# A chunked recurrence's triangular inverse: from 64x64 products to 32x32 tiles with one joining step

## What is computed

```python
def step(state, inp):
    r_t, w_t, k_t, v_t, kk_t, a_t = inp
    sa = jnp.einsum('bhvk,bhk->bhv', state, -kk_t)
    state = (state * w_t[:, :, None, :] + sa[..., None] * (kk_t * a_t)[:, :, None, :]
             + v_t[..., None] * k_t[:, :, None, :])
    return state, jnp.einsum('bhvk,bhk->bhv', state, r_t)
```

## Time and profile before

| what | value |
|---|---|
| median of 3 runs | 1946.18 us (1941.5 to 1951.0) |
| the profiled execution | 1940.98 us |
| its span, first to last instruction | 1939.2 us |
| mean granted TensorE clock in the span | 0.986 of full speed |
| TensorE busy | 1866.9 us, 96% |
| DVE, ACT, GpSimd busy | 362.0, 260.8, 49.6 us |
| matmuls, and as many weight loads | 19404 |
| from level 0 to the chunk loop, in each layer | 62.53 us |

### The profile page before, as it was taken

The page is one execution under the profiler, slowest core; times in us unless marked ns, Lnnn a source line. Parts: engine busy times, 40 slices in busy tenths (PEclk is TensorE's granted clock), DMA queues, the critical chain, the costliest instruction groups (busy, mean ns, idle before and its releaser), DMA issues.

```text
span 1939.2 us, 42075 instructions
## 1 busy us (share of the span) xinstructions
PE 1866.9 (96%) x19404; PEld 1228.6 (63%) x19404; DVE 362.0 (19%) x760; ACT 260.8 (13%) x514; POOL 49.6 (3%) x98
## 2 busy tenths in 40 slices
PE   6999999999999999999799999999999999999996
PEld 5788878788887778878535445353454535445354
DVE  1355133100001555232310101001010010100102
ACT  1324111100001333120100000100001000100001
POOL 3000200000000001100000000000000000000000
PEclk9999999999999999999799999999999999999998
DMA  6432212443434332221989999999999999999970
GB/s 189 148 130 88 89 45 87 175 172 131 171 112 132 120 108 88 89 84 48 380 335 369 363 366 416 354 373 357 356 399 369 376 357 364 387 370 389 353 267 23
DMA packets 122838, 462.08 MB, mean 238 GB/s; under 512 B 9566, under 2 KB 20496, under 8 KB 106288
## 3 DMA queue, kind: packets, MB, share of 16 engines
q1 hardware_dynamic: 122672, 459.46, 62.8%
HBM read 458.39 MB, written 1.05 MB: 237 GB/s over the span
## 4 chain that ended last, share of the span: by engine, by line
PE 96%; DVE 2%; ACT 1%; DMA 1%; issue 1%; SPq 0%; DVEq 0%; ACTq 0%
PE bank L1002 30%; PE bank L383 25%; PE bank L1028 15%; PE bank L885 4%; PE bank L675 3%; PE bank L845 3%; PE bank L958 2%; PE bank L716 2%; PE bank L832 1%; PE bank L967 1%; PE bank L1013 1%; PE bank L422 1%; PE bank L369 1%; DMA slot<-in_ffn_w_gate 0%; PE bank L759 0%
## 5 line engine op out<-in xcount | busy, mean ns | idle before, releaser
L1002 PE MATMUL bank<-slot,xg 128*32 128x512 f32 (+1 forms) x6144 | 582.1, 539 | 0.0
L383 PE MATMUL bank<-h,slot 128*128 128x256 f32 x2176 | 486.5, 383 | 7.5 <-ACT rel L1454 5.3
L383 PEld LDWEIGHTS bank<-h,slot 128*128 128x128 f32 x2176 | 414.0, 192 | 70.0 <-issue 13.7
L1002 PEld LDWEIGHTS bank<-slot,xg 128*32 128x32 f32 x6144 | 198.4, 110 | 371.0 <-issue 368.9
L1028 PE MATMUL bank<-slot,aT 128*32 128x256 f32 x5376 | 293.4, 379 | 0.0
L1028 PEld LDWEIGHTS bank<-slot,aT 128*32 128x32 f32 x5376 | 173.4, 110 | 115.0 <-issue 2.7
L2125 DVE TENSOR_TENSOR av<-gs,bank 128x512 f32<-128x512 f32 (+1 forms) x48 | 29.8, 621 | 618.2 <-PE bank L1002 618.2
L885 PE MATMUL bank<-hid,slot 128*128 128x256 f32 x352 | 77.0, 379 | 0.9 <-DVE hid L1992 0.9
L885 PEld LDWEIGHTS bank<-hid,slot 128*128 128x128 f32 x352 | 66.9, 190 | 10.2 <-issue 1.2
L1593 ACT ACTIVATE gs<-bank 128x512 f32<-128x512 f32 (+1 forms) x48 | 25.2, 543 | 284.6 <-PE bank L1002 284.5
L1599 ACT ACTIVATE aT<-bank 128x512 f32<-128x512 f32 (+1 forms) x48 | 23.2, 544 | 288.9 <-PE bank L1013 288.9
(11 more groups left out here) (400 smaller groups left out, 1190.3 us busy)
## 6 DMA issues: line engine op xcount, KB each, us to landing
slot<-in_moe_w_gate SPq DMA_DIRECT2D x32, 2048.0 KB, 11.6
slot<-in_moe_w_up SPq DMA_DIRECT2D x32, 2048.0 KB, 15.5
slot<-in_moe_w_down SPq DMA_DIRECT2D x32, 2048.0 KB, 10.6
slot<-in_moe_w_gate SPq DMA_DIRECT2D x32, 1536.0 KB, 7.7
slot<-in_moe_w_up SPq DMA_DIRECT2D x32, 1536.0 KB, 11.6
slot<-in_moe_w_down SPq DMA_DIRECT2D x32, 1536.0 KB, 8.5
slot<-in_w_in SPq DMA_DIRECT2D x20, 2048.0 KB, 8.2
slot<-in_ffn_w_gate SPq DMA_DIRECT2D x5, 2048.0 KB, 7.8
```

The costliest lines, as they stand in the source:

```text
L383: ins = mm(o, w[:, k, c:c + n], rhs[:, k, :], start=k == 0, stop=k == nk - 1)
L1002: ins = mm(banks[b0 + g][32 * p:32 * p + 32, 0:width], xg[:, k, 32 * g:32 * g + 32], w[:, kk, p * width:(p + 1) * width], start=k == 0, st ...
```

## The change

The inverse up to blocks of 32 (levels 0 to 4) is kept compactly. A 64x64 chunk inverse has, up to that level, only two 32x32 diagonal blocks, so Ti, Tt and Xs become [128, 16, 32]: partitions in quarters of 32, 16 = 2 token tiles x 8 heads. `blocks` makes a product for both token tiles at once in one bank: 16 x 4 matmuls of 32x32, quarter r of the partitions with quarter r of the output. In level 0, x0 and y0 are Lo's blocks against a 32x32 identity and the other way about. Levels 1 to 4 have x, z and y as before, with the gate halves where they were. Lo keeps its full width, and GpSimd's masks of a level now wait for one bank (y0, then x) and TensorE for both masks.

Level 5 becomes the join: `xl` multiplies the off-diagonal 32x32 block of Bm with Ti, 32 matmuls over two banks; ACT and DVE evacuate one bank each; then the first filler; then `zl`, 32 matmuls over two banks, from Xs and Tt. The wide result Tf is put together from clears (GpSimd, twice, in level 0), copies of Tt (GpSimd twice, ACT once, DVE once) and the two evacuations of zl, and TensorE waits for all of these ahead of the chunk loop. SA reads Tf in place of Tt. The set-up makes a 32x32 identity in four more copies.

The core of the diff (left out: the places of the tiles and the semaphore's name):

```diff
@@ -675,15 +677,29 @@
                             ins = mm(b[hs(q), m * HC:(m + 1) * HC], lhs(q, m), rhs(q, m), start=True, stop=True)
                     close_bank(ins, name)
 
-                for lev in range(NLEV):
-                    for tt in range(NT):
-                        need(pe, "lo_ready", (l * NLEV + lev) * NT + tt + 1)
-                        if lev:
-                            for nm in ("y", "z") if lev > 1 else ("x",):
-                                need_sb(pe, f"{l}{nm}{lev - 1}{tt}")
-                        product(f"{l}x{lev}{tt}", tt, lambda q, m: Lo[hs(q), tt, m, :],
-                                lambda q, m: Ti[hs(q), tt, m, :] if lev else id64[hs(q), :])
+                def quarter(r):
+                    return slice(32 * r, 32 * r + 32)
+
+                def low(r, n):
+                    c = 32 * (r % 2)
+                    return Lo[quarter(r), n // 8, n % 8, c:c + 32]
+
+                def blocks(name, lhs, rhs):
+
+                    b = open_bank(pe, name)
+                    for n in range(16):
+                        for r in range(4):
+                            ins = mm(b[quarter(r), 32 * n:32 * n + 32], lhs(r, n), rhs(r, n), start=True, stop=True)
+                    close_bank(ins, name)
+
+                def one(r, n):
+                    return ident[quarter(r), 32 * r:32 * r + 32]
+
+                for lev in range(NLEV - 1):
+                    need(pe, "lo_ready", (l * (NLEV - 1) + lev + 1) * NT)
                     if lev == 0:
+                        blocks(f"{l}x0", low, one)
+                        blocks(f"{l}y0", one, low)
                         for tt in range(NT):
                             need_sb(pe, f"{l}vt{tt}")
                             for g in range(2):
...
@@ -692,17 +708,24 @@
                             product(f"{l}Gv{tt}", tt, lambda q, m: Bm[hs(q), tt, m // 4, m % 4, 2, :],
                                     lambda q, m: vt[hs(q), tt, head(m // 4, m % 4)])
                         continue
-                    if lev < NLEV - 1:
-                        gate_half(5 + lev, 0)
-                    for tt in range(NT):
-                        need_sb(pe, f"{l}x{lev}{tt}")
-                        product(f"{l}z{lev}{tt}", tt, lambda q, m: Xs[hs(q), tt, m, :],
-                                lambda q, m: Tt[hs(q), tt, m, :])
-                        if lev < NLEV - 1:
-                            product(f"{l}y{lev}{tt}", tt, lambda q, m: Tt[hs(q), tt, m, :],
-                                    lambda q, m: Xs[hs(q), tt, m, :])
-                    if lev < NLEV - 1:
-                        gate_half(5 + lev, 1)
+                    need_sb(pe, f"{l}x0" if lev == 1 else f"{l}y{lev - 1}")
+                    blocks(f"{l}x{lev}", low, lambda r, n: Ti[quarter(r), n, :])
+                    gate_half(5 + lev, 0)
+                    need_sb(pe, f"{l}x{lev}")
+                    need_sb(pe, f"{l}y0" if lev == 1 else f"{l}z{lev - 1}")
+                    blocks(f"{l}z{lev}", lambda r, n: Xs[quarter(r), n, :], lambda r, n: Tt[quarter(r), n, :])
+                    blocks(f"{l}y{lev}", lambda r, n: Tt[quarter(r), n, :], lambda r, n: Xs[quarter(r), n, :])
+                    gate_half(5 + lev, 1)
+                need_sb(pe, f"{l}y{NLEV - 2}")
+                need_sb(pe, f"{l}z{NLEV - 2}")
+                xb = [open_bank(pe, f"{l}xl{q}") for q in range(2)]
+                for n in range(16):
+                    for q in range(2):
+                        ins = mm(xb[q][quarter(2 * q + 1), 32 * n:32 * n + 32],
+                                 Bm[quarter(2 * q), n // 8, n % 8 // 4, n % 4, 0, 32:HC], Ti[quarter(2 * q), n, :],
+                                 start=True, stop=True)
+                        if n == 15:
+                            close_bank(ins, f"{l}xl{q}")
 
                 wb = c3(open_slot(pe, L + "pa"), 4, D)
 
...
@@ -731,10 +754,20 @@
                     if not fill:
                         free_slot(L + "pa", f"{l}pd3")
 
+                filler()
+                need_sb(pe, f"{l}xl0")
+                need_sb(pe, f"{l}xl1")
+                zb = [open_bank(pe, f"{l}zl{q}") for q in range(2)]
+                for n in range(16):
+                    for q in range(2):
+                        ins = mm(zb[q][quarter(2 * q), 32 * n:32 * n + 32], Xs[quarter(2 * q + 1), n, :],
+                                 Tt[quarter(2 * q + 1), n, :], start=True, stop=True)
+                        if n == 15:
+                            close_bank(ins, f"{l}zl{q}")
+                need(pe, "t_copied", 6 * (l + 1))
+                need_sb(pe, f"{l}zl0")
+                need_sb(pe, f"{l}zl1")
                 for tt in range(NT):
-                    if tt == 0:
-                        filler()
-                    need_sb(pe, f"{l}z{NLEV - 1}{tt}")
                     need_sb(pe, f"{l}Gv{tt}")
                     need_sb(pe, f"{l}bt{tt}")
                     need_sb(pe, f"{l}kt{tt}")
...
@@ -756,7 +789,7 @@
                     b = open_bank(pe, f"{l}SA{c}")
                     for u in range(2):
                         for j in range(4):
-                            ins = mm(b[hs(q), col(u, j)], Tt[hs(q), tt, 4 * u + j, :],
+                            ins = mm(b[hs(q), col(u, j)], Tf[hs(q), tt, 4 * u + j, :],
                                      Gs[hs(q), col(u, j)] if c else Gv[hs(q), tt, col(u, j)], start=True, stop=True)
                     close_bank(ins, f"{l}SA{c}")
                     if c < NC - 1:
...
@@ -1317,6 +1350,9 @@
                     step(nc.gpsimd.tensor_copy(tri[64:128, i, :], tri128[64:128, i % 2, 64:128]))
                 step(nc.gpsimd.tensor_copy(id64[0:64, :], ident[0:64, 0:64]))
                 step(nc.gpsimd.tensor_copy(id64[64:128, :], ident[64:128, 64:128]))
+                for r in range(4):
+                    o = slice(32 * r, 32 * r + 32)
+                    step(nc.gpsimd.tensor_copy(id32[o, :], ident[o, o]))
                 for lv in range(NLEV):
                     bs = 1 << lv
                     o = lev128[:, lv, :].rearrange("p (n b) -> p n b", b=2 * bs)[:, :, bs:]
...
@@ -1350,19 +1386,30 @@
                     need_sb(gp, f"{l}vt{tt}")
                 for g in range(2):
                     need_sb(gp, f"{l}bo{g}")
-                for lev in range(NLEV):
+                for lev in range(NLEV - 1):
                     for tt in range(NT):
                         if lev == 0:
                             for g in range(2):
                                 for u in range(2):
                                     need_sb(gp, f"{l}B{tt}{g}{u}")
                         elif lev == 1:
-                            need_sb(gp, f"{l}x0{tt}")
+                            take(gp, f"{l}y0")
                         else:
-                            take(gp, f"{l}x{lev - 1}{tt}")
+                            take(gp, f"{l}x{lev - 1}")
                         nc.gpsimd.tensor_tensor(Lo[:, tt, :, :], Bm[:, tt, :, :, 0, :].rearrange("p u j t -> p (u j) t"),
                                                 level[:, lev:lev + 1, :].broadcast_to([P, 8, HC]),
                                                 ALU.mult).then_inc(S["lo_ready"], 1)
+                    if lev == 0:
+                        need(gp, "lo_ready", l * (NLEV - 1) * NT + NT)
+                        for q in range(2):
+                            nc.gpsimd.memset(Tf[64 * q + 32:64 * q + 64, :, :, 0:32], 0.0).then_inc(S["t_copied"], 1)
+                        need(gp, "t_copied", 6 * l + 2)
+                need_sb(gp, f"{l}z{NLEV - 2}")
+                need(gp, "lo_ready", (l + 1) * (NLEV - 1) * NT)
+                for q in range(2):
+                    o = slice(64 * q, 64 * q + 32)
+                    nc.gpsimd.tensor_copy(Tf[o, :, :, 0:32].rearrange("p t m c -> p (t m) c"),
+                                          Tt[o, :, :]).then_inc(S["t_copied"], 1)
 
             need(gp, "x_ready", 4)
             nc.gpsimd.memset(Ys[:, :, :], 0.0).then_inc(S["ys_act"], 1)
...
@@ -1528,11 +1575,16 @@
                 gate_out(5)
                 for tt in range(NT):
                     evac(f"{l}Gv{tt}", Gv[:, tt, :])
-                for lev in range(1, NLEV):
-                    for tt in range(NT):
-                        evac(f"{l}x{lev}{tt}", Xs[:, tt, :, :], lambda b: b[:, :].rearrange("p (m t) -> p m t", m=8))
-                    if lev < NLEV - 1:
-                        gate_out(5 + lev)
+                def m16(b):
+                    return b[:, :].rearrange("p (n t) -> p n t", n=16)
+
+                for lev in range(1, NLEV - 1):
+                    evac(f"{l}x{lev}", Xs[:, :, :], m16)
+                    gate_out(5 + lev)
+                evac(f"{l}xl0", Xs[32:64, :, :], lambda b: m16(b)[32:64])
+                need_sb(act, f"{l}z{NLEV - 2}")
```

(44 more changed lines are left out.)

10 lines of the change are left out of this document (6 added, 4 removed).

## The result

The change made the kernel slower: 1973.15 us (median of 4 runs, 1967.95 to 1980.81) against 1944.01 (4 runs, 1941.5 to 1951.0), ratio 1.015 [1.0127, 1.0173]. The interval of the ratio leaves out 1, so the slowdown of 1.5% is clear of noise. The forecast was 1910.5 with a range to 1930. The profiled execution of after took 1980.81 us, 39.8 more than that of before, and is the slowest of its four; the medians differ by 29.1.

The account below looks back on a forecast made before the run. TensorE's own time in small matmuls was taken as the bound. A layer's window of 256r + 36.8 us, 44.7 at r = 31 ns, saved 17.8, two layers 35.7, giving 1910.5 us from a median of 1946.18; range 1903 to 1930.

Parts of the forecast that it names:

- the number of matmuls in a layer's inverse does not: Each layer's inverse: 960 matmuls before and after, only more sharing a round: 64 in 16 rounds of four.
- 36.8: Window from level 0 to the chunk loop: the us a layer added to 256 rounds of length r.
- Nobody is waited for. The time is TensorE's own: Old kernel's levels: evacuations, additions and masks all end under a gate half of 3.65 us, so small-matmul pace decides.
- rival B: Inverse's small matmuls: no cheaper at 32 columns, a round stays 57.4 ns, 22.1 us saved, 1924.1; chance 0.34.
- SP gains no DMA: Weight loads: no DMA added; p_fox and p_dsa land 11.2 and 13.3 us after sending, filler some 19 away.
- The round of four: Inverse: four 32x32 tiles run side by side, estimated at 31 ns a round, bounds 26.7 to 115.
- Rival D: Inverse: four row groups of one bank take turns, 230 ns a round, 27.6 us lost a layer, 2001; chance 0.04.
- rival C: Inverse: four tiles keep 28.7 ns a matmul, 115 a round, 1950, no change; chance 0.10 with what lies around it.
- rival B's second reading: TensorE's feed gives out at 15.6 ns a matmul with its load, 62 a round; would save 19.7 us.
- The join: Tail replacing level 5: 3.96 us against 5.80, saved 1.8, including a new wait of 0.9 before the chunk loop.
- The clears and copies of Tf: GpSimd, ACT and DVE: put at nothing, covered by other work; GpSimd's four uncovered would be 5.5 us a layer.
- GpSimd's masks as a stall of 1.3 us in level 0: Level 0: Gv no longer covers level 1's masks, TensorE idles about 1.3 us; level takes 4.13, a loss of 0.4.

Follow-up runs that it names:

- e1: Changed kernel with half the matmuls in levels 1 to 4, each weight block running over 64 columns: 1925.01 us (one run), before 1941.63.
- f3: Changed kernel, same matmul count, each matmul of levels 1 to 4 running over 64 columns, the next overwriting half: 1975.59 us (one run), before 1943.45.
- e2: Changed kernel with the loads of p_fox and p_dsa cut to 64 of 1024 columns: 1965.26 us (one run).
- f4: Changed kernel with p_fox and p_dsa loaded ahead of the last gate weights, these held back until gate unit 9 is done: 1968.79 us, ratio 1.0133.
- e3: Changed kernel with y0 made by four matmuls of 512 columns instead of 64 over 32: 1965.93 us, ratio 1.0124.
- f1: Changed kernel with wide y0, p_fox and p_dsa loaded before the last gate weights, and gate matmuls inside x, z and y: 1961.39 us, ratio 1.0088.
- g2: Changed kernel with wide y0 and p_fox and p_dsa loaded before the last gate weights, without gate matmuls between small ones: 1957.27 us, ratio 1.0063.
- e4: Changed kernel with three of the second gate half's eight matmuls put between the halves of z and y: 1966.72 us, ratio 1.0127.
- g1: Kernel before with four 64x64 tiles side by side, earlier level-1 masking and level 5 waiting for one Xs at a time: 1932.43 us against 1941.55, ratio 0.9949.

## Why the prediction was wrong

**The count of matmuls, the step that failed first.** The prediction took a `product` to be 32 matmuls in the source, said that before and after have 960 a layer and that "the number of matmuls in a layer's inverse does not" change. In the source a `product` is 8 heads x 2 chunks = 16; the text ahead of the prediction has the same error where it writes 8 heads x 2 chunks = 32. Each float32 matmul stands in the trace as two MATMUL and two LDWEIGHTS instructions, so the 32 instructions of a row are 16 matmuls, while the 64 of `blocks` were read from the source and become 128. Before has 30 x 16 = 480 matmuls a layer, after 14 x 64 + 64 = 960: 960 instructions became 1920. The page says so, 19404 to 21324, which is 1920 in two layers. The prediction named "19404 matmuls as before" as the thing to look for, and that is the row that fails. With the right count a layer has 512 rounds: 512 x 0.0335 + 36.8 = 54.0 us, 8.5 saved, 17 in all. On that step alone the forecast would have been 1929 instead of 1910.5, still faster and still inside the range. So this step doesn't explain the result; the next one does.

**What gave the result its sign: TensorE's instructions.** The prediction wrote "Nobody is waited for. The time is TensorE's own" and kept that for the new kernel: it costed matmuls by time in the array only and put the supply of instructions at nothing. It did name the feed, in rival B, but as a pace of 15.6 ns a matmul; what the trace shows is full pace up to the end of a packet and then a halt of 1.3 to 5 us. e1 and f3 show that the count decides. The halts are 16.0 and 15.8 us a window. One packet after another needed 3.45 to 3.74 us with hardly any weight transfers during the halt (e2) and 6.2 with them during the halt (after, f3), and the new stream uses one up in 1.1. The Trainium skill, Runtime: NRT & Kernel Launch, section Instruction fetch mechanics, says that instructions are fetched in blocks of 16 KiB, 256 of them, and that crossing a block is mostly hidden. The trace agrees on the size (2.77 MB in 169 packets) and not on the hiding: here the halts stand at the crossings.

**The clock.** The prediction took 1.00 from the earlier trace rows as given. The granted clock fell to 0.89 and 0.79, where TensorE had stood before. What is left of the windows when the 54.0 and the halts are taken off, 77.57 - 54.0 - 16.0 = 7.6 and 82.86 - 54.0 - 15.8 = 13.1, is put down to it by subtraction. Rows of the timeline carry most of it. In layer 0 the slower gate halves have 5.1 (5.30, 5.84, 5.04 and 3.82 against 3.72) and the Gv product behind the first halt 1.5 (3.37 us at a clock of 0.55, against 1.86). In layer 1 the gate halves of 3.88, 6.05, 6.71, 6.44 and 5.30 have 9.8, Gv 1.7 (3.61 at 0.50) and x of level 1 another 0.5 (1.85 at 0.50 against 1.35). The 54.0 also holds a wait of 1.3 for GpSimd's masks that this kernel didn't have, so what is left is 1.3 more in each layer, and some 2 us a layer have no row of their own. No run kept the halts and held the clock; that the clock's fall goes with the halts is shown (e1: 0.97 and 1.00). The four shares together are -17.1, 31.8, 20.7 and 4.4 outside the windows, the 39.8 of the profiled executions.

**The transfers.** "SP gains no DMA" was right, and nothing waited for p_fox or p_dsa. The filler stood 35 us behind their issue (235.44 to 270.47) and not 19, because the halts had stretched the window. That they would lie on top of a shortage of instructions and double one halt a layer was not seen; e2 and f4 show it. The text ahead of the prediction puts "pa" in the slot of gate units 6 and 7. It takes that of gate units 4 and 5 and stands in SP's queue behind the load of the last gate weights, which waits for unit 7: the time of its issue, 235.44, is as said, for another reason.

**What held.** The round of four, 31 ns forecast and 33.6 measured. Rival D, four row groups of one bank taking turns at 230 ns, is refuted by the same rows; the Trainium skill, TensorEngine Tiling (Array Packing), section Restrictions and Gotchas, says that different row tiles cannot use one bank at the same time, and at 33.6 ns for four of them this trace disagrees. So does e1: with 64 columns four row tiles of one bank take 57 ns a round, no longer than the two of before. Rival B's 57.4 a round and rival C's 115 are refuted too as paces; rival B's second reading, the feed, pointed at the right place with the wrong price. The join was right in place and size: xl at 269.34, filler at 270.47, zl at 272.39, and then the new wait ahead of the chunk loop, 0.97 us where 0.9 was forecast. The timeline of after there (PE):

```profile
269.34 1.20 PE L724 MATMUL bank<-Ti,Bm 32*32 32x32 f32 x64
270.47 1.99 PE L739 MATMUL bank<-oF,slot 128*128 128x256 f32 x8
272.39 1.20 PE L763 MATMUL bank<-Tt,Xs 32*32 32x32 f32 x64
274.56 1.05 PE L792 MATMUL bank<-Gv,Tf 64*64 64x64 f32 x15 [0.97 <-DVE Tf L1947]
```

The join took 5.22 us where 3.96 was forecast, again by the count: xl and zl have 32 rounds each and not 16, and 64 x 0.0335 + 2.97 is 5.1. The clears and copies of Tf cost nothing, as said. GpSimd's masks as a stall of 1.3 us in level 0 did not appear, because Gv ran at near half speed above them (3.28 us for its 64 weight loads); in e3, f1 and g2, which have no halt in y0, TensorE waits 0.69 to 0.70 us for them.

**What stays open.** What makes TensorE's queue ask for its next packet, and how far ahead, no run tells. That halts fall on multiples of 128 matmul instructions was read from the traces afterwards and not forecast for any kernel. How the clock's fall grows with the halts is open as well: f1, with 4.2 us of them a window, had 0.95, as e4 had in layer 0 with 10.1.

## What to carry to other kernels

Before a change cuts matmuls into smaller ones, count instructions in the trace's own unit, on both sides of the change, and check one source line's count against its row. Then set the instructions of the stretch against how many packets of them it got before: here a stream that ran through 256 in 1.1 us stood still between packets, and one that took 1.8 us for them (f3) still did. Faster tiles bring nothing in such a stretch. Look first for a placement that fills more of the array with the instructions already there, as g1 does.
